# Mixer 1 fed chunk by chunk: query latents, modulation, squares and small weights moved about

## The reference

```python
f1 = swiglu(rms_norm(h, ffn1_pre_g), gate1, up1, down1)        # D_FF = 2816
h = h + 0.5 * rms_norm(f1, ffn1_post_g)
u = rms_norm(h, mix_pre_g)
cq, ckv, kr, dq, dk, dv, g = split(u @ w_in)                   # 384, 256, 32, 3 x 512, 2048
q = rms_norm(cq, q_norm_g) @ w_uq; c_kv = rms_norm(ckv, kv_norm_g)  # then attentions, gates, w_out
h = h + rms_norm(mix, mix_post_g)
f2 = swiglu(rms_norm(h, ffn2_pre_g), gate2, up2, down2)
h = h + 0.5 * rms_norm(f2, ffn2_post_g)
```

## Time and profile before

| | us |
|---|---|
| three runs | 1343.4, 1348.06, 1351.78 |
| median | 1348.06 |
| the profiled execution | 1338.22 |
| its span | 1336.6 |
| PE busy in the span | 1261.7 |
| DVE, ACT, POOL busy | 790.7, 593.2, 451.5 |
| mean granted clock of PE | 0.967 |

### The profile page before, as it was taken

The page is one execution under the profiler, slowest core; times in us unless marked ns, Lnnn a source line. Parts: engine busy times, 40 slices in busy tenths (PEclk is TensorE's granted clock), DMA queues, the critical chain, the costliest instruction groups (busy, mean ns, idle before and its releaser), DMA issues.

```text
span 1336.6 us, 23437 instructions
## 1 busy us (share of the span) xinstructions
PE 1261.7 (94%) x8728; PEld 1144.8 (86%) x8728; DVE 790.7 (59%) x1133; ACT 593.2 (44%) x976; POOL 451.5 (34%) x252
## 2 busy tenths in 40 slices
PE   4999999988999999999999999998999997999998
PEld 4999999966887999999998878876546797999998
DVE  5577773854874556766453844576323584655555
ACT  4444445524661454444534544344203533655553
POOL 0244434731560533333354642121000374122221
PEclk8999997988999999999969999999999999999999
DMA  8677763422333446777503323222212254455553
GB/s 256 221 280 264 271 218 111 140 96 101 106 111 124 161 172 241 263 264 271 187 30 124 116 94 127 79 81 84 88 63 94 65 174 142 138 180 186 178 183 110
DMA packets 64124, 206.98 MB, mean 155 GB/s; under 512 B 12736, under 2 KB 14400, under 8 KB 63936
## 3 DMA queue, kind: packets, MB, share of 16 engines
q1 hardware_dynamic: 49824, 177.23, 39.2%
q0 software_dynamic: 6912, 25.17, 5.3%
q10 hardware_dynamic: 7328, 3.74, 1.1%
HBM read 205.07 MB, written 1.05 MB: 154 GB/s over the span
## 4 chain that ended last, share of the span: by engine, by line
PE 78%; DVE 11%; ACT 4%; issue 3%; DMA 2%; ACTq 1%; POOL 1%; DVEq 0%; SPq 0%; POOLq 0%
PE psum L591 18%; PE psum L592 17%; PE psum L593 17%; PE psum L562 8%; PE psum L1191 2%; PE psum L916 2%; PE psum L721 2%; DMA low<-stream 2%; PE psum L612 1%; DVE high L2009 1%; ACT parts L1386 1%; PE psum L1056 1%; DVE parts L1978 1%; POOL own_parts L2673 1%; DVE high L2150 1%
## 5 line engine op out<-in xcount | busy, mean ns | idle before, releaser
L591 PE MATMUL psum<-parts 128*128 128x256 f32 x1584 | 453.2, 286 | 18.5 <-DVE parts L1978 9.3
L592 PE MATMUL psum<-parts 128*128 128x256 f32 x1584 | 451.1, 285 | 0.0
L593 PE MATMUL psum<-parts 128*128 128x256 f32 x1584 | 451.0, 285 | 0.0
L591 PEld LDWEIGHTS psum<-parts 128*128 128x128 f32 x1584 | 307.4, 194 | 20.8 <-issue 13.1
L592 PEld LDWEIGHTS psum<-parts 128*128 128x128 f32 x1584 | 307.2, 194 | 0.0
L593 PEld LDWEIGHTS psum<-parts 128*128 128x128 f32 x1584 | 307.0, 194 | 0.0
L1386 ACT ACTIVATE parts<-low 128x1024 fp32r<-128x1024 f32 x198 | 207.9, 1055 | 201.6 <-DMA low<-stream 198.3
L2681 POOL TENSOR_TENSOR parts<-low,parts 128x1024 fp32r<-128x1024 f32 x60 | 156.7, 2612 | 366.6 <-ACT parts L1386 366.6
L2673 POOL TENSOR_TENSOR own_parts<-low,parts 128x1024 fp32r<-128x1024 f32 x76 | 186.9, 2470 | 209.7 <-ACT parts L1453 205.3
L1978 DVE TENSOR_TENSOR parts<-low,parts 128x1024 fp32r<-128x1024 f32 x138 | 174.3, 1266 | 102.8 <-ACT parts L1386 102.5
L562 PE MATMUL psum<-low 128*128 128x256 f32 (+1 forms) x512 | 132.1, 412 | 1.2 <-ACT high L1466 1.2
(11 more groups left out here) (342 smaller groups left out, 1917.8 us busy)
## 6 DMA issues: line engine op xcount, KB each, us to landing
low<-stream SPq DMA_DIRECT2D x334, 512.0 KB, 3.5
high<-conditioning POOLq DMA_DIRECT2D x48, 512.0 KB, 5.0
low<-x SPq DMA_DIRECT2D x4, 256.0 KB, 5.5
high<-ctx ACTq DMA_DIRECT2D x1, 1024.0 KB, 6.2
out<-low SPq DMA_DIRECT2D x8, 128.0 KB, 1.8
low<-cst ACTq DMA_DIRECT2D x1, 850.5 KB, 5.9
high<-wuq ACTq DMA_DIRECT2D x1, 768.0 KB, 12.6
high<-wuq ACTq DMA_DIRECT2D x1, 384.0 KB, 13.7
```

The source lines that it names most:

```text
L591: pe.matmul(out, w_hi[:, cols_], x_hi, start=start, stop=False, **kw)
L592: pe.matmul(out, w_hi[:, cols_], x_lo, start=False, stop=False, **kw)
L593: return pe.matmul(out, w_lo[:, cols_], x_hi, start=False, stop=stop, **kw)
```

## The change

It has five parts. The first: `wuq` is loaded in one plain load, and DVE pulls the heads apart with two copies behind the scaling of `kv_norm`; PE waits for them before `uq0`. The second: after feed-forwards 1 and 2, DVE first adds the squares in pairs, so PE has four chunks to sum instead of eight. The third: the three query tiles are worked together, chunk by chunk, into banks 4, 5 and half of bank 0 (`ckv0` into half of bank 1), as `input_parts` counts; the modulation moves behind `dq3`, its copy and the small vectors on DVE behind the weight copies. The fourth: the inversions of `mix_pre` and `kv_norm` stand inside DVE's angle steps, uppers and lowers of mixer weights move forward. The fifth: in the feed-forwards the hidden chunk 0 is split ahead of tile 6, and in feed-forward 2 tiles 4 and 5 are split after the inversion.

```diff
 # PE
             add_eps("ffn1_post", "ffn1_pre", 1)
-            for n in range(DC):
-                squares_ready("ffn1_post", n // 2 + 1)
-                add_squares("ffn1_post", sq[:, n, :], False, n == DC - 1)
+            for n in range(4):
+                square_sum_ready("ffn1_post", "square_sums_2", 1 + n // 2)
+                add_squares("ffn1_post", sq[:, 4 * (n // 2) + n % 2, :], False, n == 3)
             spread("ffn1_post")
-            modulation(0, 0, 0, 24)
...
-            for n in range(3):
-                split_project(f"cq{n}", chunk_ready=lambda k: pe.wait_ge(S("input_parts"), INPUT_PARTS["mix_pre"] + k + 1))
+            latent_banks = {"cq0": bank("cq0")[:, 0:T], "cq1": bank("cq1")[:, 0:T], "cq2": half_bank(0, 0),
+                            "ckv0": half_bank(1, 0), "ckv1": bank("ckv1")[:, 0:T]}
+            queries = [split_weights(AT[("cq", n)]) for n in range(3)]
+            for k in range(DC):
+                pe.wait_ge(S("input_parts"), INPUT_PARTS["mix_pre"] + k + 1)
+                if k == 0:
+                    pe.wait_ge(S("post_scaled"), 4)
+                for n in range(3):
+                    mm = split_product(latent_banks[f"cq{n}"], queries[n], slice(k * P, (k + 1) * P),
+                                       (p1_hi[:, k, :], p1_lo[:, k, :]), k == 0, k == DC - 1)
+                    if k == DC - 1:
+                        mm.then_inc(S("tiles_used"), 1)
+            split_cols(tile_of("ckv0"), latent_banks["ckv0"], lambda k: p1_hi[:, k, :], lambda k: p1_lo[:, k, :])
...
             split_project("dq3")
+            modulation(0, 0, 0, 24)
             spread("kv_norm")
             bank_free(pe, "kr")
-            pe.wait_ge(S("small_weights"), 48)
+            pe.wait_ge(S("small_weights"), 32)
...
             pe.wait_ge(S("q_scaled"), 3)
+            pe.wait_ge(S("kv_scaled"), 4)
...
-            for n in range(DC):
-                squares_ready("ffn2_post", n // 2 + 1)
-                add_squares("ffn2_post", sq_late[:, n, :], False, n == DC - 1)
+            for n in range(4):
+                square_sum_ready("ffn2_post", "square_sums_2", 4 + n // 2)
+                add_squares("ffn2_post", sq_late[:, 4 * (n // 2) + n % 2, :], False, n == 3)
 # ACT
                 for par in range(2):
                     gate(par, par, k > 0, 0)
+                    if par == 0:
+                        upper_hidden(par, FC * k + par)
+                        if k == 1:
+                            upper(1, 5)
                     upper(k, 6 + 3 * par)
-                    upper_hidden(par, FC * k + par)
+                    if par == 1:
+                        upper_hidden(par, FC * k + par)
...
-            w_heads = dram["wuq"].rearrange("p k (h c) -> p (k h) c", h=HEADS)
-            for part, own in ((w_nope, slice(0, NOPE)), (w_rope, slice(NOPE, NOPE + ROPE_D))):
-                act.dma_start(part.rearrange("p k (h c) -> p (k h) c", h=HEADS),
-                              w_heads[:, :, own]).then_inc(S("small_weights"), 16)
+            act.dma_start(wuq, dram["wuq"]).then_inc(S("small_weights"), 16)
...
             post_squares(0)
+            weight_upper(AT[("cq", 0)] + 3)
             take_root_deferred("ffn1_post")
...
                 if n == 5:
-                    weight_upper(AT[("cq", 0)] + 3)
+                    weight_upper(AT[("cq", 0)] + 4)
...
-            uppers(1, 4, RING)
             act.preload_act_table(ACT.Silu)
             copy_inverse("ffn2_pre", inv)
+            upper(1, 4)
 # DVE
+            def pair_sums(name, x):
+                for i in (0, 2):
+                    dve.wait_ge(S("squares"), SQ_BASE[name] + i + 2)
+                    dve.tensor_tensor(x[:, 2 * i:2 * i + 2, :], x[:, 2 * i:2 * i + 2, :], x[:, 2 * i + 2:2 * i + 4, :],
+                                      ALU.add).then_inc(S("square_sums_2"), 1)
...
+            pair_sums("ffn1_post", sq)
             post("ffn1_post", lambda n: input_lower_1(n - 3) if n >= 3 else None)
...
-            mod_copy(0, 24, 0, 1)
...
-            for part in two_pi_parts():
+            for i, part in enumerate(two_pi_parts()):
                 link(dve.scalar_tensor_tensor(out=ang, in0=turns, scalar=-part, in1=ang, op0=ALU.mult, op1=ALU.add))
+                if i == 1:
+                    invert("kv_norm")
...
+            dve.wait_ge(S("small_weights"), 32)
+            w_heads = wuq.rearrange("p k (h c) -> p (k h) c", h=HEADS)
+            for part, own in ((w_nope, slice(0, NOPE)), (w_rope, slice(NOPE, NOPE + ROPE_D))):
+                dve.tensor_copy(part.rearrange("p k (h c) -> p (k h) c", h=HEADS), w_heads[:, :, own])\
+                   .then_inc(S("kv_scaled"), 1)
+            mod_copy(0, 24, 0, 1)
...
-            lower(1, 4)
             invert("ffn2_pre")
-            lower(1, 5)
 # POOL
-            weights_lower(AT[("cq", 0)], AT[("cq", 0)] + 2)
+            weights_lower(AT[("cq", 0)], AT[("cq", 0)] + 3)
             add_residual(0)
+            weights_lower(AT[("cq", 0)] + 4, AT[("cq", 0)] + 4)
             pool.wait_ge(S("square_sums"), 2)
-            weights_lower(AT[("cq", 0)] + 3, AT[("g1", 13)])
+            weights_lower(AT[("cq", 0)] + 5, AT[("g1", 13)])
```

More of the change, by code:

```diff
@@ L1936, in scale_into @@
             def scale_into(name, dst, src, g, sem, between=lambda n: None, inv_=inv):
[L1938 removed]
+                if name not in ("q_norm", "kv_norm"):
                     invert(name)
@@ L2046, in multiply @@
                        .then_inc(S("gates_scaled"), 1)
+                    if k == 1 and isinstance(f, int) and f == 0:
+                        lower(1, 4)
                     dve.wait_ge(S("silus"), f + (FC * k + 1))
```

64 lines of the change are left out of this document (35 added, 29 removed).

## The result

| | before | after |
|---|---|---|
| runs compared | 5 | 5 |
| median, us | 1345.4 | 1334.2 |
| lowest to highest | 1342.2 to 1351.8 | 1325.9 to 1335.5 |
| the profiled execution | 1338.22 | 1325.86 |
| its span | 1336.6 | 1324.2 |

The ratio is 0.9898, with an interval of 0.9857 to 0.9940: about 1% faster. The time is inside the range that was given (1311 to 1339), but outside the 1320 to 1332 that the forecast itself stood for: 1334 is where its rivals 1 and 2 lay (1335). The two medians differ by 11.2 us and the two profiled executions by 12.4, and the forecast was 21.9. About half of the gain that was counted did not come, and this part is about that half.

A forecast was written before the change was run, and what follows sets the result against it. PE was busy 94% of the span, so gains had to come from its idle time, low-clock matmuls or waits; 10.2 + 9.8 + 1.6 + 0.3 = 21.9 us off 1348.06 gave 1326 us, range 1311 to 1339.

The forecast's parts named there:

- Rival 1: Only the mixer half comes: ACT still waits at its queue, or the position table takes over; 1335 us, 10%.
- Rival 2: Only the start comes: bunched loads, late splits, POOL in DVE's way, clock staying at 0.50; 1335 us, 10%.
- A: Feed-forward 1's start: plain load of `wuq` frees ACT's queue, first "down" at 26.0 instead of 36.2; gain 10.2 us.
- B: Mixer 1: shorter sums, query tiles worked together, modulation moved behind dq3; `kr` ends 9.8 us earlier.
- The sums: Mixer 1's start: fewer matmuls for the squares' sums, spread ends near 221.3 instead of 224.3; gain 3.0 us.
- the query latents: Mixer 1: three query tiles done at 234.4 instead of 244.15; together with the sums 9.7 us.
- From there to the end of dq3: Mixer 1 after the query tiles: PE's 20.1 us without a wait are kept, so dq3 ends at 254.6.
- the residuals' parts: Mixer 1's last two input parts: slowed beside POOL, they come at 232.3 and 232.7, not 230.7; PE wants them at 232.4.
- rival 4: Mixer 1: DVE's chain to the `kr` product makes `rdq0` wait 38 us; net 16 lost, 1364 us, 3%.
- The modulation's place: Mixer 1 behind dq3: its 6.3 us fill PE's idle time waiting for kv_norm's inversion, so the move costs nothing.
- C: Feed-forward 2's start: inversion first and hidden chunk split earlier, "down" at 485.0 instead of 486.65; gain 1.6 us.
- D: Sums after feed-forward 2: DVE's addition slowed beside POOL's lowers; gain 0.3 us, 3.0 if the two did not meet.

The follow-up runs named there:

- the two freed kernels: Kernels before and after, each with POOL's lowers of feed-forward 1 cut from 1024 to 64 columns: 1334.3 us (ratio 0.9942) and 1326.6 us (0.9879).
- plain_alone: Kernel before with only the load of `wuq` in one piece and DVE's two copies in mixer 1: 1336.3 us, ratio 0.9947.
- q_first: Kernel after with DVE's inversion of q_norm moved ahead of the two steps that make `turns`: 1324.3 us, ratio 0.9842.
- The freed kernel before: Kernel before with POOL's lowers of feed-forward 1 cut to 64 columns: 1334.3 us, ratio 0.9942.
- mod_back: Kernel after with the modulation put back ahead of the latents: 1337.9 us, ratio 0.9967.
- zeroed_lowers: Kernel after with POOL's subtraction for five weight tiles of mixer 1 replaced by filling the lower parts with zeros: 1328.2 us, ratio 0.9883.
- three_moves: Kernel after with q_first's move, the position conversion moved to mixer 1, and `wuq`/`wkr` loads moved to feed-forward 1's end: 1325.8 us, ratio 0.9881.

## Why the prediction was right and where it was wrong

**A, 10.2 forecast.** The steps up to the first "down" held: `wuq`'s issue 0.67 for 0.5 (`wkr` 1.09), spread at 20.0 for 20.1, "down" at 26.4 for 26.0, idle 2.8 for 2.6. The drop of the clock, which I had kept as a bound, came: it stood at 0.50 from 26 to 29. The failing step is unwritten: I took the gain at the first "down" for the gain at the end of feed-forward 1. In the profiled executions 7.8 arrived, 4.8 in the two freed kernels, 7 (4 to 10) in the runs of plain_alone. In the profiled pair neither tiles nor rhythm took the missing 2.0 us: behind the first "down" PE waits 2.2 us in both kernels. Some 1.4 of it is the clock, which stood at 0.50 while PE did the first 12 matmuls of that tile in 2.9 us (0.12 each at full clock), and the rest is open. With the 2.4 that I had written as the bound for this the forecast would have been 7.8, which is what came; that it fits so well is luck. In other executions two more things eat it: weight tiles that the full DMA engines have not brought yet, and the loop's rhythm. Rival 1 in its first form is out: the same 1.15 MB that took 0.68 and 9.36 us to issue in two loads of short runs took 0.67 in one of long runs, and `wkr` behind it 1.09 instead of 2.52. Whether the length of the runs or the number of loads does it, no run here separates.

**B, 9.8 forecast, 5.2 measured; 4 to 5 come back with one line moved, by the checkpoints.** The sums gave 2.4 for 3.0, and by the end of the query latents 9.5 of 9.7 was there. The step that failed is "From there to the end of dq3, PE did 20.1 us without a wait. I keep that." PE waited 3.8 us for q_norm's inversion, and the clock fell behind it (dq2 4.3 us, in q_first 3.05). By the sign that the prediction gave itself (wrong if PE stands between dq1 and `rdq0` for more than 3 us in all) it was wrong here, though the time fell into the range. The trace of before would have told, in lines that I did not read, DVE's timeline of it:

```profile
245.26 0.17 DVE L1930 RECIPROCAL high<-high 128x2 f32<-128x2 f32 x1 [4.00 <-ACT high L1348]
...
255.45 0.17 DVE L1930 RECIPROCAL high<-high 128x2 f32<-128x2 f32 x1
```

PE wanted that spread at 257.6, so the margin was 2.1 us. The change brought PE there 17.3 us earlier and the inversion, behind its steps, only 11.4 (255.45 to 244.02); the difference of 5.9, less the margin, is the wait of 3.8. It has two parts. From mix_pre's inversion to q_norm's DVE took 10.2 us before and 11.9 after (232.14 to 244.02): 1.7, as the steps had become slower, 2.5 us each for the last two `ang` where the four of before took 5.73 together, since the change releases the query tiles at once and POOL then has five lowers in a row. The other 4.2 arose further ahead: mix_pre's inversion itself came only 13.1 us earlier. PE's sum for it stands behind `ckv0` after the change, and stood ahead of `ckv0` before, one tile (3.0 us) later by the order of the list, and ACT then took the root behind a weight's upper (1.06 us at 230.28). The forecast took neither part into its sum. Most of DVE's slowing was there in the kernel before, where the margin hid it. I had counted that slowing for the residuals' parts and in rival 4, for the product of `kr`, but not for the queue ahead of the inversion in between. The order of PE's sum was changed back in no run, so its share is read from the two traces and not shown by an experiment. The modulation's place was right: its 5.5 us (forecast 6.3) cover kv_norm, and without it 7.8 us are lost.

**C, 1.6 forecast:** 1.5 by the checkpoints; the waits there fell from 2.8 us to 1.1, by 1.7, and came back when it was undone. **D, 0.3 forecast:** the addition took 2.55 for the 2.7 foretold, gain 0.2; undone, nothing was lost. POOL's lowers do stand in its way.

**The baseline.** I put the median 10 us above the profiled execution and carried that over. Both kernels have such a distance (7 and 8 us). The freed kernel before, 8 us faster than before, makes the loop's collisions its likely cause there; the one profiled execution of the kernel before has just two slow sums and 2.2 us of waits, so that is inferred. For the kernel after it is open: freeing the loop changed its ratio by 0.2%.

**Of the table's remainder,** 1.6 went to the clock ahead of feed-forward 2 (above), feed-forward 2 gained 1.8 more, 0.4 of it C's shorter wait for the hidden chunk, and the part behind it lost 2.7. PE's clock was 0.93 over 903 to 926 in before and 0.86 over the same work in after; nothing was run on that.

Rival 2 (only the start comes, 1335) was nearest, in time and on mechanism, since POOL did get in DVE's way, but mixer 1 gave half and not nothing. That the time lies in the range is owed to the range's width, and not to the sum.

## What to carry to other kernels

When a step is moved so that an engine gets somewhere earlier, list what stands in every queue ahead of each result it will now want, and cost those instructions beside whatever the shared partner (here POOL for DVE) will be doing at the new time, not at their old durations. A gain at the start of a long loop that is nearly balanced between engines is not a gain at its end: compare the loop's own length in several executions before counting on it. When the order of a list is changed, look also at what now stands one tile later than before: here it was a short sum, and everything behind its inversion moved with it. By the checkpoints, a one-line move of a short instruction ahead of long ones was worth about as much (4.9 us) as all the restructuring of mixer 1 had brought (5.2).

## What was not expected of the hardware

A loop of fixed work took 188 to 205 us with its POOL instructions whole, and executions in which this loop's code is the same differ by 13.5 us (after 190.0, mod_back 203.5). The longest are those in which POOL's lower (2.4 us and more) falls on DVE's sums most often: 13 of 40, at 3.4 us instead of 1.2. DVE's slowing does not need a large instruction: one over 128x2 took 1.61 us instead of 0.14 (L1948 in after and in zeroed_lowers). DVE's steps ended within 0.3 us of POOL's instructions, while reciprocals (0.17, at 232.14) and products from PSUM (0.42, at 149 us of three_moves) beside one were not touched.
